# Index stacks issued from two queues, top-k and splits spread over the attention units, and dummy products in its short units

## The chip, the cores and the metric

One core of a Trainium2 chip runs the whole program as one launch. The metric is the device time of one execution in microseconds; lower is better.

## What is computed

Two blocks on 512 tokens of width 1024, in float32. The first block has two layers of feed-forward, hybrid mixer, output product and feed-forward, each with a layer norm; the second is a Mamba-2 and RG-LRU block with a feed-forward. The change touches the hybrid mixer alone, which runs once in each of the two layers. Of it, cut to what matters here:

```python
def dsa_mixer(q, k, v, q_idx, k_idx, w_idx, ...):      # per block of 128 queries
    rel = jax.nn.relu(jnp.einsum('bqhd,bsd->bqhs', qi, k_idx))   # 8 index heads of 32
    score = jnp.einsum('bqh,bqhs->bqs', wi, rel)
    score = jnp.where(k_pos <= q_pos, score, NEG_INF)
    _, idx = lax.top_k(score, 128)                      # then attention on the chosen keys
...
y = concatenate([mla(...), nsa(...), dsa(...), stick_breaking(...)])   # 4 heads of 64 each
```

## The kernel before

Every large product is made of three float32r products: a high part (`whi`, copied by ACT, L314) and a low part (`wlo`, subtracted on DVE, L318) of the weights, which come through a ring of four `raw` buffers that SP loads (L302). One weight tile is a slot. PE's slot needs both parts of its tile, and ACT and DVE make those of slot n+2 while PE works on slot n.

**The front** (`mixer_front`, phase "proj") has 20 slots: 12 feature tiles, 4 token tiles (12 to 15), and 4 feature tiles (16 to 19) whose matmuls (L1058 to L1060) (24 a slot) are interleaved with index scores (L1030, 6 a slot, 24 in all): stack of head h by `kstack`, then a relu on ACT (L1147) into `rel`, then a weighted sum on DVE (L1223, L1227) into `picked` (named idx_score in the trace). For each of the 8 index heads the stack holds four copies of 32 rows, high, low, high, low, of the rotated queries; SP makes them with four transfers a head, 32 in a layer (L931): heads 0 to 3 at its step 12, heads 4 to 7 at its step 14. `rel` lies on the memory of the queries' high parts, so the first relu waits until the second half of the stacks has landed (`istack_in1`). The first half must have landed before PE's first index product. In its last two slots ACT and DVE also make the high and low parts of the next phase's first two tiles, and DVE ends with three additions of the causal mask to the score blocks (L1252).

**Attention** (`mixer_attention`, phase "att") is a list of 20 groups of 4 units (heads), 80 units, in the order of `ORDER`; a unit belongs to one of five kinds and one block of 128 queries. On every unit the engines do, each in its own order: PE the scores of unit u+2 (L1370, mask L1371), the transposes of unit u (L1380), the values of u-1 (L1391); DVE the row minimum of u+2 (L1560); ACT the exponential of u+1 (L1472) and the copy of the transposed probabilities of u (L1481). PE's `transposes(u)` waits first for `pt_done`, the copy of unit u-1, then for `exp_done`; on ACT that copy comes behind the exponential of u. 16 steps of stick-breaking attention (L1408 to L1429) are spread over the units. DVE also makes the 48 top-k rounds, one each on units 0 to 47, in the order of blocks 1, 2, 3: `max` finds the eight largest (L1537), `match_replace` takes them out (L1544). ACT and DVE split 12 operand tiles into high and low parts, one a unit on units 0 to 11 (L1457, L1459; L1597, L1600). A block's choice is needed by its DSA group: block 2 at unit 48, block 3 at 64, block 1 at 76. Units of a "cmp" group have a width of 31 keys, those of block 0 a width of 128. `keep_clock` (L369) exists and isn't called before the change.

Of the kernel before, what the change touches and what calls it, by code (L numbers as in the profile page):

```python
# [7 lines left out]
F32 = mybir.dt.float32  # L8
# [6 lines left out]
P = 128  # L15
# [826 lines left out]
def mixer_front(c, m, l, following):  # L842
# [24 lines left out]
    index = (IDXK, IDXQ, IDXQ + 1)  # L867
# [8 lines left out]
    def halves(lo, hi, dim):  # L876

        half = dim // 2
        return [(a, a + half if (a - lo) // half % 2 == 0 else a - half, half) for a in range(lo, hi, half)]

# [5 lines left out]
    with ExitStack() as ctx:  # L886
# [5 lines left out]
        with nc.Block() as block:  # L892
            @block.sync
            def _(sp):
# [40 lines left out]
                for n in range(slots):  # L935
# [31 lines left out]
                    if n == 14:  # L967
# [3 lines left out]

                        sp.wait_ge(ph["gelu_done"], 2)
                        stack(1)
# [6 lines left out]
            def _(pe):  # L980
# [89 lines left out]
                for n in range(2, slots):  # L1070
# [14 lines left out]
            def _(act):  # L1085
# [41 lines left out]
                def index_hi(i):  # L1127
                    if i == 0:
                        act.wait_ge(ph["idxk_in"], 64)
                    else:  # L1130
                        act.wait_ge(ph["rope_done"], parts[order.index(4 + i) + 1])
                    hi, _, src, _ = m.split[index[i]]
                    act.activation(hi, src, ACT.Copy).then_inc(ph["ihi_done"], 1)
                    if i == 0:
                        act.wait_ge(ph["copies_in"], 16 * 6)
                        act.activation(kstack[0:64], src[0:64], ACT.Copy).then_inc(ph["ihi_done"], 1)

                def relus(n):
                    for i in rels_of(n):
# [4 lines left out]
                        if i >= 3:  # L1144
# [6 lines left out]
                          11: lambda: (index_hi(2), gelus()), 12: compressed}  # L1151
                act.nop().then_inc(ph["bank_free"], 4)
                apply.act(act)
                for n in range(slots):
# [4 lines left out]
                    ph.hi(act, n // 4, n % 4, width(n + 2), last=n >= slots - 4)  # L1159
# [4 lines left out]
            def _(dve):  # L1164
# [36 lines left out]
                def index_lo(i):  # L1201
                    dve.wait_ge(ph["ihi_done"], i + 2)
                    hi, lo, src, _ = m.split[index[i]]
                    if i == 0:
# [27 lines left out]
                for n in range(slots):  # L1232
# [5 lines left out]
                    ph.lo(dve, n // 4, n % 4, width(n + 2), last=n >= slots - 4)  # L1238
# [10 lines left out]
                dve.wait_ge(ph["acc_done"], len(rels))  # L1249
# [1337 lines left out]
```

## Time and profile before

| | |
|---|---|
| median of 3 runs | 3546.96 us (3545.58 to 3554.99) |
| the profiled execution's own time | 3556.16 us |
| its span | 3554.3 us |
| mean granted TensorE clock | 0.967 of full |
| fronts: layer 0, layer 1 | about 400 to 555 us, about 1553 to 1709 us |
| attention: layer 0, layer 1 | about 555 to 724 us, about 1709 to 1871 us |

The span runs from the first to the last instruction that the profile shows; the execution's own time has 1.9 us around it. A granted clock of 1.00 is 2.4 GHz on TensorE, 0.50 is 1.2 GHz. Attention is counted here from ACT's first copy of transposed probabilities to its last: 560.92 to 724.05 us and 1714.24 to 1870.84 us. Unit 8 of layer 1 begins by the same mark at 1732.24 us, unit 48 at 1814.88 us. A matmul's end is modelled, so a matmul that is issued every 0.22 us is shown as lasting 0.39 us.

### The profile page before, as it was taken

How to read it: one execution, taken by the hardware profiler on the slowest of the kernel's cores; microseconds unless marked ns; L12 is line 12 of the kernel's file. 1: busy time of each engine (PE TensorE's matmuls, PEld its weight loads, DVE VectorE, ACT ScalarE, POOL GpSimd, SP SyncE). 2: the span in 40 equal slices, each digit the busy share in tenths (PEclk: the TensorE clock that was granted, in tenths of full speed). 3: DMA queues.
4: the chain of work that ended last, by engine and by line, in shares of the span. 5: the costliest groups of instructions: out<-in, count | busy, mean ns of one | idle time of the engine just before them, and what ended most of it. 6: DMA issues, size and time to landing. Idle time of an engine off the chain costs nothing. (4 is left out here: it accounts for less than half of the span.)

```text
span 3554.3 us, 41810 instructions
## 1 busy us (share of the span) xinstructions
PE 3322.8 (93%) x15368; PEld 2671.0 (75%) x15370; DVE 1642.7 (46%) x2465; ACT 1413.4 (40%) x2342; POOL 77.5 (2%) x52
## 2 busy tenths in 40 slices
PE   7999988989999999999898999979999899889998
PEld 5887776768888788777676888847777677768886
DVE  3333457753333433345865333366566346343333
ACT  4332436544322433243665332245555237233321
POOL 0001000010001000100001000100000000000000
PEclk9999998999999999999999999989999999999999
DMA  3232240012232233224001223211111222222231
GB/s 133 97 107 98 90 121 24 1 60 89 95 106 85 74 96 103 98 90 122 24 1 60 95 99 104 81 56 55 55 66 61 76 81 103 77 72 99 94 107 65
DMA packets 85880, 286.34 MB, mean 81 GB/s; under 512 B 15841, under 2 KB 19425, under 8 KB 85217
## 3 DMA queue, kind: packets, MB, share of 16 engines
q1 hardware_dynamic: 85728, 284.37, 24.3%
q8 instruction: 89, 1.46, 0.2%
q14 instruction: 63, 0.51, 0.0%
HBM read 269.12 MB, written 2.10 MB: 76 GB/s over the span
## 5 line engine op out<-in xcount | busy, mean ns | idle before, releaser
L318 DVE TENSOR_TENSOR wlo<-raw,whi 128x1024 fp32r<-128x1024 f32 (+3 forms) x464 | 609.3, 1313 | 989.0 <-ACT whi L314 988.8
L346 PE MATMUL ps<-xh,whi 128*128 128x512 f32 x2256 | 886.1, 393 | 16.7 <-DVE xl L2535 6.3
L347 PE MATMUL ps<-xl,whi 128*128 128x512 f32 x2256 | 880.1, 390 | 0.0
L348 PE MATMUL ps<-xh,wlo 128*128 128x512 f32 x2256 | 879.9, 390 | 0.0
L314 ACT ACTIVATE whi<-raw 128x1024 fp32r<-128x1024 f32 (+3 forms) x464 | 515.0, 1110 | 657.6 <-PE ps L348 614.3
L346 PEld LDWEIGHTS ps<-xh,whi 128*128 128x128 f32 x2256 | 425.2, 188 | 114.8 <-issue 25.1
L348 PEld LDWEIGHTS ps<-xh,wlo 128*128 128x128 f32 x2256 | 425.0, 188 | 88.7
L347 PEld LDWEIGHTS ps<-xl,whi 128*128 128x128 f32 x2256 | 425.1, 188 | 88.6 <-issue 1.7
L346 PE MATMUL ps<-ffn_hh,whi 128*128 128x512 f32 x880 | 347.2, 395 | 11.1 <-DVE ffn_hl L751 11.1
L347 PE MATMUL ps<-ffn_hl,whi 128*128 128x512 f32 x880 | 345.1, 392 | 0.0
L348 PE MATMUL ps<-ffn_hh,wlo 128*128 128x512 f32 x880 | 345.0, 392 | 0.0
L706 ACT ACTIVATE ffn_hh<-ffn_gate 128x512 f32 (+1 forms) x110 | 69.6, 633 | 512.0 <-DVE ffn_gate L749 512.0
L749 DVE TENSOR_TENSOR ffn_gate<-ffn_gate,ps 128x512 f32<-128x512 f32 x110 | 75.7, 688 | 282.6 <-PE ps L348 282.6
L346 PEld LDWEIGHTS ps<-ffn_hh,whi 128*128 128x128 f32 x880 | 166.8, 189 | 48.8 <-DVE ffn_hl L751 13.2
L347 PEld LDWEIGHTS ps<-ffn_hl,whi 128*128 128x128 f32 x880 | 166.8, 190 | 35.5 <-issue 1.0
L348 PEld LDWEIGHTS ps<-ffn_hh,wlo 128*128 128x128 f32 x880 | 166.7, 189 | 35.0
L1950 PE MATMUL ps<-xh,whi 128*128 128x512 f32 x384 | 159.9, 416 | 15.8 <-PEq L297 15.8
L702 ACT ACTIVATE ffn_gate<-ps 128x512 f32<-128x512 f32 x110 | 65.9, 599 | 257.1 <-PE ps L348 254.4
L1951 PE MATMUL ps<-xl,whi 128*128 128x512 f32 x384 | 152.8, 398 | 0.0
L1952 PE MATMUL ps<-xh,wlo 128*128 128x512 f32 x384 | 152.5, 397 | 0.0
L509 POOL TENSOR_TENSOR x<-x,mean_rest 128x512 f32<-128x512 f32 x48 | 77.3, 1644 | 2173.0 <-ACT mean_rest L473 2173.0
L751 DVE TENSOR_TENSOR ffn_hl<-ffn_gate,ffn_hh 128x512 f32 (+1 forms) x110 | 76.2, 693 | 98.8 <-ACT ffn_hh L706 98.8
(393 smaller groups left out, 4095.5 us busy)
## 6 DMA issues: line engine op xcount, KB each, us to landing
raw<-in_ffn_up SPq DMA_DIRECT2D x216, 512.0 KB, 3.5
raw<-in_ffn_down SPq DMA_DIRECT2D x80, 704.0 KB, 4.0
raw<-in_ssm_in SPq DMA_DIRECT2D x44, 512.0 KB, 3.5
raw<-in_mix_in SPq DMA_DIRECT2D x32, 512.0 KB, 3.6
raw<-in_lru_in SPq DMA_DIRECT2D x20, 512.0 KB, 3.6
raw<-in_mix_out SPq DMA_DIRECT2D x16, 512.0 KB, 3.7
raw<-in_ssm_out SPq DMA_DIRECT2D x16, 512.0 KB, 3.5
raw<-in_lru_out SPq DMA_DIRECT2D x8, 640.0 KB, 3.9
```

Of the source, the lines that this page charges most:

```text
L314: act.activation(self.core.whi[:, u % HALF, 0:width], self.core.raw[:, u, 0:width], ACT.Copy).then_inc(sems["hi_done"], 1)
L318: dve.tensor_tensor(self.core.wlo[:, u % HALF, 0:width], self.core.raw[:, u, 0:width], self.core.whi[:, u % HALF, 0:width].bitcast(F32), A ...
L346: pe.matmul(out, c.whi[:, h, w], xh[:, k0 + k], start=first and k == 0, stop=False)
L347: pe.matmul(out, c.whi[:, h, w], xl[:, k0 + k], start=False, stop=False)
L348: mm = pe.matmul(out, c.wlo[:, h, w], xh[:, k0 + k], start=False, stop=last and k == nk - 1)
L509: pool.tensor_tensor(c.x[:, t], c.x[:, t], c.dneg[:], ALU.add).then_inc(ph["xc_done"], 1)
L706: act.activation(hh[:, p], gate[:, u // 2], ACT.Copy).then_inc(ph["hh_done"], 1)
L749: dve.tensor_tensor(gate[:, u // 2], gate[:, u // 2], c.ps[:, u], ALU.mult).then_inc(ph["prod_done"], 1)
L751: dve.tensor_tensor(hl[:, p], gate[:, u // 2], hh[:, p].bitcast(F32), ALU.subtract).then_inc(ph["hl_done"], 1)
L1950: pe.matmul(out, c.whi[:, h, w], c.xh[:, t], start=t == 0, stop=False)
L1951: pe.matmul(out, c.whi[:, h, w], c.xl[:, t], start=False, stop=False)
L1952: mm = pe.matmul(out, c.wlo[:, h, w], c.xh[:, t], start=False, stop=t == DT - 1)
```

## The change

It lets ACT issue the stacks of heads 0 to 3 (one at its step 12, two at 13, one at 14) and SP those of heads 6, 7, 4, 5 (steps 12, 13, 14), and splits the index queries before the index key. It leaves out the next phase's first two tiles in the front's last two slots and makes them on attention's units 34 and 36. It moves the three mask additions to units 3, 5 and 7. It takes the top-k blocks in the order 2, 3, 1, with the 48 rounds spread evenly over units 9 to 70. It keeps the first seven splits on units 0 to 6 and puts the other five on units 20, 23, 26, 29 and 31. And it puts dummy products (bf16, 512 columns) into `transposes`, between its two waits: two on a unit with a width under 128, one on a unit with a width of 128.

```diff
-    index = (IDXK, IDXQ, IDXQ + 1)
+    index = (IDXQ, IDXQ + 1, IDXK)
 ...
+    def stack_head(engine, h):
+        hi, lo = m.split[IDXQ + h // 4][:2]
+        rows = slice(32 * (h % 4), 32 * (h % 4) + 32)
+        for g in range(4):
+            engine.dma_start(stack_of[h][32 * g:32 * g + 32].bitcast(F32), (hi, lo)[g % 2][rows, P:SEQ].bitcast(F32)).then_inc(ph[f"istack_in{h // 4}"], 16)
 ...
-                def stack(i):
-                    sp.wait_ge(ph["ilo_done"], i + 2)
-                    t = IDXQ + i
-                    hi, lo = m.split[t][0], m.split[t][1]
-                    for h in range(4):
-                        rows = slice(32 * h, 32 * h + 32)
-                        for g in range(4):
-                            sp.dma_start(stack_of[4 * i + h][32 * g:32 * g + 32].bitcast(F32), (hi, lo)[g % 2][rows, P:SEQ].bitcast(F32)).then_inc(ph[f"istack_in{i}"], 16)
+                def stack(heads):
+                    for h in heads:
+                        stack_head(sp, h)
 ...
                     if n == 12:
-                        sp.wait_ge(ph["km_done"], HEADS)
-                        sp.wait_ge(ph["vm_done"], 2)
-                        stack(0)
                         sp.wait_ge(ph["rope_done"], parts[order.index(9) + 1])
                         for a in (0, 64):
                             sp.dma_start(m.h[a:a + 64, KWIN], m.h[64:P, KSLC]).then_inc(ph["kwin_in"], 16)
 ...
                     if n == 14:
                         sp.wait_ge(ph["kwin_in"], 32)
                         sp.dma_start(m.h[64:P, KSLC], m.h[0:64, KSLC]).then_inc(ph["kslc_in"], 16)
+                        stack((4, 5))
+                    if n == 12:
+                        sp.wait_ge(ph["ilo_done"], 2)
+                        stack((6,))
+                    if n == 13:
                         sp.wait_ge(ph["gelu_done"], 2)
-                        stack(1)
+                        stack((7,))
 ...
-                            pe.wait_ge(ph["ilo_done"], 1)
+                            pe.wait_ge(ph["ilo_done"], 3)
 ...
+                def stack(h):
+                    act.wait_ge(ph["ilo_done"], 1)
+                    act.wait_ge(ph["km_done"], HEADS)
+                    act.wait_ge(ph["vm_done"], 2)
+                    stack_head(act, h)
 ...
-                          11: lambda: (index_hi(2), gelus()), 12: compressed}
+                          11: lambda: (index_hi(2), gelus()), 12: lambda: (compressed(), stack(0)),
+                          13: lambda: (stack(1), stack(2)), 14: lambda: stack(3)}
 ...
-                    ph.hi(act, n // 4, n % 4, width(n + 2), last=n >= slots - 4)
+                    if n + 2 < slots:
+                        ph.hi(act, n // 4, n % 4, width(n + 2))
 ...
-                    ph.lo(dve, n // 4, n % 4, width(n + 2), last=n >= slots - 4)
+                    if n + 2 < slots:
+                        ph.lo(dve, n // 4, n % 4, width(n + 2))
 ...
-                dve.wait_ge(ph["acc_done"], len(rels))
-                for b in range(1, QB):
-                    own = m.picked[b][:, b * P:(b + 1) * P]
-                    dve.tensor_tensor(own, own, c.k["negd"], ALU.add).then_inc(ph["acc_done"], 1)
 ...
-    rounds = [(b, r) for b in range(1, QB) for r in range(TOPK // 8)]
+    chosen = (2, 3, 1)
+    rounds = [(b, r) for b in chosen for r in range(TOPK // 8)]
+    round_at = {9 + k * (n - 19) // (len(rounds) - 1): k for k in range(len(rounds))}
+    done_at = {b: max(u for u, k in round_at.items() if rounds[k][0] == b) for b in chosen}
 ...
+    part_at = dict(zip((0, 1, 2, 3, 4, 5, 6, 20, 23, 26, 29, 31), range(len(parts))))
+    ahead_at = {34: 0, 36: 1}
 ...
-                    for b in range(1, QB):
+                    for b in chosen:
                         if u == first_unit[2, b]:
-                            pe.wait_ge(ph["choice_done"], b)
+                            pe.wait_ge(ph["choice_done"], chosen.index(b) + 1)
 ...
                     if u >= 1:
                         pe.wait_ge(ph["pt_done"], u)
+                    keep_clock(c, pe, T_BANK, 2 if x["width"] < P else 1 if x["width"] == P else 0)
                     pe.wait_ge(ph["exp_done"], u + 1)
 ...
-                    if u < len(parts):
-                        hi(u)
+                    if u in part_at:
+                        hi(part_at[u])
+                    if u in ahead_at:
+                        ph.split_hi(act, c.sides[0], 0, ahead_at[u], D)
 ...
+                def own_block(b):
+                    own = picked[b][:, b * P:(b + 1) * P]
+                    dve.tensor_tensor(own, own, c.k["negd"], ALU.add).then_inc(ph["own_done"], 1)
 ...
-                    largest()
+                    if u in (3, 5, 7):
+                        own_block((3, 5, 7).index(u) + 1)
+                    if u in round_at:
+                        largest(round_at[u])
                     if u % HEADS == 1 and u > HEADS:
                         finish(u // HEADS - 1)
-                    take()
-                    if u < len(parts):
-                        lo(u)
-                    allow()
+                    if u in round_at:
+                        take(round_at[u])
+                    if u in part_at:
+                        lo(part_at[u])
+                    if u in ahead_at:
+                        ph.split_lo(dve, c.sides[0], 0, ahead_at[u], D)
+                    if u in round_at:
+                        allow(round_at[u])
```

## Rows read from the trace of the kernel before

**Rows 1.** The page, part 1: busy time and share of the span by engine.

```profile
PE 3322.8 (93%) x15368; PEld 2671.0 (75%) x15370; DVE 1642.7 (46%) x2465; ACT 1413.4 (40%) x2342; POOL 77.5 (2%) x52
```

**Rows 2.** Waits from 330 to 560 us: who waited for whom, total, times, longest.

```profile
ACT idx_rel L1147 <- DMA idx_stack<-mix_h_split: 11.9, 1, 11.9
...
PE ps L1030 <- ACT idx_rel L1147: 8.8, 1, 8.8
```

**Rows 3.** Timeline of the SP queue, layer 0: start us, us, engine, line, transfer.

```profile
499.16 0.51 SPq L931 DMA_DIRECT2D idx_stack<-index_hi  x1
...
508.58 0.59 SPq L931 DMA_DIRECT2D idx_stack<-mix_h_split  x1
...
514.00 1.78 SPq L931 DMA_DIRECT2D idx_stack<-index_hi  x1
...
523.43 0.59 SPq L931 DMA_DIRECT2D idx_stack<-mix_h_split  x1
```

**Rows 4.** Transfers into idx_stack: min, median and max from issue to landing.

```profile
DMA to landing us min/median/max: 1.9/1.9/3.5
```

**Rows 5.** Timeline of ACT, front of layer 0.

```profile
502.24 0.99 ACT L314 ACTIVATE whi<-raw 128x936 fp32r<-128x936 f32 x1 [4.57 <-PE ps L1044]
...
512.48 1.06 ACT L314 ACTIVATE whi<-raw 128x1024 fp32r<-128x1024 f32 x1 [4.06 <-PE ps L1044]
...
530.85 0.60 ACT L1158 ACTIVATE mix_h<-ps 128x512 f32<-128x512 f32 x1 [1.96 <-PE ps L1060]
...
550.69 0.60 ACT L1158 ACTIVATE mix_h<-ps 128x512 f32<-128x512 f32 x1 [0.76 <-PE ps L1060]
```

**Rows 6.** Timeline of PE, the same stretch.

```profile
513.02 0.39 PE L1059 MATMUL ps<-xl,whi 128*128 128x512 f32 x1
513.24 0.39 PE L1060 MATMUL ps<-xh,wlo 128*128 128x512 f32 x1
...
525.86 0.69 PE L1030 MATMUL ps<-idx_kstack,idx_stack 128*128 128x384 f32 x1 [8.79 <-ACT idx_rel L1147]
```

**Rows 7.** Windows at half clock: us, busy PE, PEld, DVE, ACT, POOL; clock, DMA share, GB/s.

```profile
526.00:531.00 5.00, 5.00 (x12) 3.98 (x13) 2.81 (x6) 2.08 (x6) 0.00 (x0) 0.50 0.49 186
583.00:597.00 14.00, 14.00 (x62) 12.16 (x62) 8.98 (x31) 6.56 (x23) 0.00 (x0) 0.50 0.05 11
1771.00:1780.00 9.00, 9.00 (x43) 8.14 (x43) 7.05 (x23) 3.68 (x15) 0.00 (x0) 0.50 0.01 2
```

**Rows 8.** Timelines of DVE and ACT at the front's end and after it.

```profile
511.81 2.30 DVE L1214 COPY mix_tok_sb<-ps 128x468 f32<-128x468 f32 x4
...
553.40 0.69 DVE L1252 TENSOR_TENSOR idx_score<-idx_score,consts_sb 128x128 f32<-128x128 f32 x3
...
555.49 1.28 ACT L1509 ACT_TABLE_LOAD   x1 [3.26 <-PEq L297]
```

**Rows 9.** Windows of attention: both layers, then layer 1 in three parts.

```profile
560.92:724.05 163.13, 148.83 (x966) 123.02 (x966) 118.09 (x340) 98.46 (x314) 0.00 (x0) 0.90 0.03 8
1714.24:1870.84 156.60, 141.83 (x966) 116.79 (x966) 117.87 (x340) 98.12 (x314) 0.00 (x0) 0.95 0.03 8
1714.24:1732.24 18.00, 14.58 (x87) 9.81 (x86) 17.48 (x49) 14.80 (x43) 0.00 (x0) 0.97 0.13 31
1732.24:1814.88 82.64, 73.67 (x505) 62.10 (x506) 75.89 (x221) 47.82 (x156) 0.00 (x0) 0.93 0.03 8
1814.88:1870.84 55.96, 53.58 (x375) 44.88 (x375) 24.50 (x72) 35.49 (x118) 0.00 (x0) 0.97 0.00 1
```

**Rows 10.** Top-k instructions on idx_score (ns min/median/max), and one split on DVE.

```profile
L1537 DVE MAX8 idx_top<-idx_score x96: 371/552/696, 560.8 to 1814.4; 128x8 f32<-128x256 f32 x32, 128x8 f32<-128x384 f32 x32, 128x8 f32<-128x512 f32 x32
...
L1544 DVE MATCH_REPLACE8 idx_score<-idx_top,idx_score x96: 408/542/678, 561.4 to 1815.2; 128x256 f32<-128x256 f32 x32, 128x384 f32<-128x384 f32 x32, 128x512 f32<-128x512 f32 x32
...
568.92 0.69 DVE L1597 SCALAR_TENSOR_TENSOR mix_h_split<-mix_h,query_stack 64x512 fp32r<-64x512 f32 x1
```

**Rows 11.** Waits in layer 1's attention.

```profile
PE ps L1380 <- ACT att_pt L1481: 11.0, 16, 1.7
```

More of the change, by code:

```diff
@@ L1127, in index_hi @@
                 def index_hi(i):
-                    if i == 0:
+                    hi, _, src, _ = m.split[index[i]]
+                    if index[i] == IDXK:
                         act.wait_ge(ph["idxk_in"], 64)
                     else:
-                        act.wait_ge(ph["rope_done"], parts[order.index(4 + i) + 1])
-                    hi, _, src, _ = m.split[index[i]]
+                        act.wait_ge(ph["rope_done"], parts[order.index(5 + i) + 1])
                     act.activation(hi, src, ACT.Copy).then_inc(ph["ihi_done"], 1)
-                    if i == 0:
+                    if index[i] == IDXK:
                         act.wait_ge(ph["copies_in"], 16 * 6)
                         act.activation(kstack[0:64], src[0:64], ACT.Copy).then_inc(ph["ihi_done"], 1)
+                def stack(h):
[3 more added lines that the diff above has]
+                    stack_head(act, h)
                 def relus(n):
@@ L1201, in index_lo @@
                 def index_lo(i):
-                    dve.wait_ge(ph["ihi_done"], i + 2)
+                    dve.wait_ge(ph["ihi_done"], i + 1)
                     hi, lo, src, _ = m.split[index[i]]
-                    if i == 0:
+                    if index[i] == IDXK:
                         hi, lo, src = hi[64:P], kstack[64:P], src[64:P]
@@ L1320, in mixer_attention @@
         first_unit.setdefault(g["mixer"], HEADS * k)
-    assert all(first_unit[2, b] >= b * (TOPK // 8) + 4 for b in range(1, QB)), "one round a unit"
+    assert len(round_at) == len(rounds) and all(first_unit[2, b] >= done_at[b] + 4 for b in chosen), "the choice comes in time"
     shortened = lambda x: x["width"] < P
@@ L1336, in mixer_attention @@
                    "gexp_done gsum_done gates_done pt_done pv_done part_done y_done top_done took_done choice_done "
-                   "zero_done nsaq_in dsaq_in z_done abs_done e_done l_done spraw_done sp_done after_done a_done spv_done sy_done")
+                   "own_done zero_done nsaq_in dsaq_in z_done abs_done e_done l_done spraw_done sp_done after_done a_done spv_done sy_done")
         with nc.Block() as block:
@@ L1528, in _, with largest, take, allow @@
             def _(dve):
-                took, allows = [0], [0]
-                def largest():
-                    if took[0] < len(rounds):
-                        b, r = rounds[took[0]]
-                        if took[0]:
-                            dve.wait_ge(ph["took_done"], took[0])
-                        dve.max(top8, picked[b]).then_inc(ph["top_done"], 1)
-                def take():
-                    if took[0] < len(rounds):
-                        b, r = rounds[took[0]]
-                        took[0] += 1
-                        dve.wait_ge(ph["top_done"], took[0])
-                        dve.match_replace(picked[b], top8, picked[b], TAKEN).then_inc(ph["took_done"], 1)
-                def allow():
-                    if took[0] and rounds[took[0] - 1][1] == TOPK // 8 - 1 and took[0] // (TOPK // 8) > allows[0]:
-                        b = rounds[took[0] - 1][0]
-                        allows[0] += 1
-                        dve.wait_ge(ph["took_done"], took[0])
+                def own_block(b):
+                    own = picked[b][:, b * P:(b + 1) * P]
+                    dve.tensor_tensor(own, own, c.k["negd"], ALU.add).then_inc(ph["own_done"], 1)
+                def largest(k):
+                    b, r = rounds[k]
+                    dve.wait_ge(ph["own_done"], QB - 1)
+                    if k:
+                        dve.wait_ge(ph["took_done"], k)
+                    dve.max(top8, picked[b]).then_inc(ph["top_done"], 1)
+                def take(k):
+                    b, r = rounds[k]
+                    dve.wait_ge(ph["top_done"], k + 1)
+                    dve.match_replace(picked[b], top8, picked[b], TAKEN).then_inc(ph["took_done"], 1)
+                def allow(k):
+                    b, r = rounds[k]
+                    if r == TOPK // 8 - 1:
+                        dve.wait_ge(ph["took_done"], k + 1)
                         dve.tensor_scalar(allowed[b], picked[b], TAKEN, NEG, ALU.not_equal, ALU.mult).then_inc(ph["choice_done"], 1)
```

## The prediction

> **What bounds the kernel now.** The busy shares come first: PE 93%, DVE 46%, ACT 40% [rows 1]. PE is the bound, so time can only be won where PE stands still, runs at half clock, or is paced by another engine. The waits of a mixer front name one large hole: ACT's first relu waits 11.9 us for the stack transfers, and PE's fifth index product 8.8 us for that relu [rows 2]. The SP queue says why they are late: its 32 stack issues run from 499.16 to 524.0 us, 0.63 us apart (499.16 to 508.58 is 15 steps), one of them 1.78 us long [rows 3]. A transfer lands 1.9 us after its issue, and in most cases no later [rows 4]: the issuing is slow, not the moving.
>
> What the hole costs is read on ACT. Slot 16 begins at 512.48 and ends at 530.85, 18.4 us; the next three of its sort take 6.6 each (530.85 to 550.69) [rows 5]. That is 11.8 us too much: PE stands until 525.86 [rows 6], and then works at a granted clock of 0.50 to 531 [rows 7]. Layer 1 shows the same hole in the same form.
>
> Behind the last relu the front's end is ACT's and DVE's: ACT has evacuated at 551.29 [rows 5], DVE ends the mask additions at 554.09, and attention's first ACT instruction starts at 555.49 [rows 8], 1.4 us after.
>
> Attention takes 163.1 us in layer 0 and 156.6 in layer 1 with the same instructions. In layer 1, DVE is busy 17.5 of 18.0 us in units 0 to 7, 75.9 of 82.6 in units 8 to 47, and 24.5 of 56.0 in units 48 to 79, where PE is busy 53.6 [rows 9]. So DVE paces the first 48 units and PE, with the latency of its chain through DVE and ACT, the last 32. On top, PE stands at 0.50 clock from 583 to 597 us in layer 0 and from 1771 to 1780 in layer 1 [rows 7]; layer 1 has nothing like the first stretch, which is the 6.5 us between the layers.
>
> **The change, part by part** (each layer unless said).
>
> *Stacks from two queues.* SP's share falls from 32 issues to 16. It starts as before at 499.16 and has 19 issues and one weight load left, 20 x 0.63 = 12.6 us, so it ends at 511.8, or 513.3 with 1.5 us held at the load for DVE's slot 15; landed by 515.2. The first relu then waits until 515.2 and not until 525.4. PE comes to its fifth index product at 525.86 - 8.79 = 517.07 [rows 6], so this wait is gone. What is late next is ACT. Its 16 issues have no row in this trace. From below they cost nothing, from above 1.78 us each [rows 3]; I take SP's common 0.63. ACT works about 1 us in a token slot of 5.12 (502.24 to 512.48 is two) [rows 5]. One head (2.5 us) fits into slot 12; two heads at step 13 (5.0 us behind a split that ends at 503.3) end at 508.3 and push the split of slot 16 from 507.4 (502.24 + 5.12) by 0.9 us. Behind it DVE has the low part, three query operations and the token copies that PE waits for, which begin at 511.81 [rows 8]: about 0.9 us late, and PE with them. Head 3 is issued by 511.9 and lands by 513.8, about when PE's first index product wants it. Remaining loss in slot 16: 0.4 us of today's normal restart plus 0.9, so about 1.3 of the 11.8. Gain 10.5, twice **21.0 us**. At 1.0 us an issue ACT's last stack lands near 518, and some 3 us a layer of this gain are lost; at 1.78 for all, near 530, which is 4.5 us a layer worse than today (3541 in the sum for the median). SP shows that length once, so I leave that end out of the range.
>
> The transfers themselves are the place to weigh a rule. In the 5 us behind the hole the DMA share is 0.49 [rows 7] with one queue's issues; two queues double the rate of stack issues, so the 16 engines would be near full at worst, and the landing of 1.9 us [rows 4] may grow by a microsecond, which I leave in the range. The Trainium skill ("DMA: Bandwidth & Descriptors", Issuing engines are not separate DMA queues) says that several issuers share the same 16 engines and save only the sequencer's time, usually small beside the transfer. By that rule taken strictly the front's 21.0 us would be near 0 and the sum 15 us; the trace speaks against it, because here the sequencer's time, 0.63 us an issue, is what ends last.
>
> *Moving the key's split behind the queries'* costs nothing: its low part comes at DVE's step 13 instead of 10, three slots ahead of PE's first index product, and that is its cover; were it gone, PE would wait for one operation of 0.7 us.
>
> *Front's end.* Without two splits and three additions the last work is ACT's evacuation, 551.29 instead of 554.09 [rows 5, 8]: 2.8 us, twice **5.6 us**.
>
> *Attention, rounds and splits.* A round is MAX8 plus MATCH_REPLACE8 plus some 0.09 us: 0.37 + 0.41 for block 1, 0.55 + 0.54 for block 2, 0.70 + 0.68 for block 3 [rows 10], so 0.87, 1.18 and 1.47 us. Units 0 to 7 lose 8 rounds (7.0 us) and a stacked split (two of 0.69 [rows 10], 1.4), and get three additions (0.9): DVE 17.5 to 10.0. ACT, 14.8 less 1.3 of the split, is next, with PE at 14.6 plus dummies. I take 15.3 for 18.0: gain 2.7. Units 8 to 47 change 40 rounds for 31 (8 of block 1 and one of block 3 less, 8.4 us), get the split of unit 7 (1.4) and the next phase's two (2.4): DVE 75.9 to 71.3. Units 48 to 79 get 17 rounds, 1.5 + 16 x 0.87 = 15.4: DVE 24.5 to 39.9 of 56, still under PE; a round may hold up a row minimum now and then, bounded by 0 and 15.4 us; I take 0.7, since the minimum runs two units ahead of PE's transposes.
>
> *Dummies.* 16 units of two and 16 of one, 48 a layer. A 512-column product is issued every 0.22 us (513.02 to 513.24) [rows 6], so 10.6 us of PE a layer, 1.8 of it in units 48 to 79. They stand behind the wait for ACT's copy and ahead of the one for the exponential. All of PE's waits there (11.0 us) are put down to the copy [rows 11], which comes behind the exponential on ACT, so nothing hides them at that place; they are hidden only where DVE paces the unit. They can give back what half clock costs: 6.5 us in layer 0, and in layer 1's 1771 to 1780 (layer 0 has its like) 9 us at 0.50, half of it at most, 4.5; I take 2.3, since DVE is busy 7.05 of those 9 [rows 7]. For units 8 to 47 the ends are 82.6 less the DVE relief, the clock and no price for dummies, 75.7, and PE 73.7 + 7.9 - 4.5 = 77.1 plus today's excess over the bound (82.6 - 75.9 = 6.7), 83.8. I take 81.3, nearer the second: gain 1.3. In units 48 to 79 they cost 1.8.
>
> Attention of layer 1: 2.7 + 1.3 - 0.7 - 1.8 = 1.5 us won. Layer 0: the same and the 6.5 of its first half-clock stretch, which PE's fuller units 0 to 11 should keep away: 8.0. Together **9.5 us**.
>
> **Sum:** 21.0 + 5.6 + 9.5 = 36.1 us off 3556.2, so 3520.1 for this profiled execution. It stands 9.2 us over the median of 3546.96. The half-clock stretch of 6.5 us that only one layer shows is the kind of thing that comes in some executions; the median likely has less of it, so of the median I take off 21.0 + 5.6 + 3.0 and some 3 for it: 32.6 us, **3514.4**.
>
> **Rivals.** *The clock and DVE's relief bring more:* dummies lie beside DVE-paced work and both layers run warm at unit lengths near the larger of the two engines. For it: DVE is busy 97% in units 0 to 7. Against: rows 11. Units 8 to 47 at 75.7 are 5.6 a layer better, 11.2 in all: 3503.
> *The dummies don't do what they are put there for*, or cost all 10.6 us: half clock stays and attention gains nothing or loses up to 6 a layer. For it: they sit behind the wait that binds. Then 26.6 us less 0 to 12: 3520 to 3532.
> *The front stays bound by its transfers or by ACT's issues* (1.0 to 1.5 us each, or landing slower by several microseconds): 10 to 20 of the 21 are lost, 3524 to 3535. Against: SP's steady 0.63. The Trainium skill's section on issuing engines, named above, points to this case.
> *Slower:* every round and dummy set into attention lands on the chain scores, minimum, exponential, transposes, and the early units give nothing back: 15.4 + 10.6 = 26.0 us a layer, 52.0, less the front's 26.6, so 3547 + 25 = 3572. It decides from 13.3 us of growth a layer. Against: DVE is busy 24.5 of 56 us where the rounds go, and 7 us leave units 0 to 7.
>
> **How the numbers follow.** A measurement tells 0.3%, 10.6 us, from no change: 3536.3 and 3557.6. Chances: forecast 0.60, more 0.15, dummies in vain 0.12 (0.02 of it beyond 3536), transfers or ACT's issues 0.09 (0.03 beyond), slower 0.04 (half of it past 3557.6). Faster 0.91, same 0.07, slower 0.02. The range takes the first rival to 3498 (its 3503 and the whole 4.5 of clock once more) and the dear ends to 3531.
>
> **What would show it.** Right: no wait of ACT for idx_stack above 2 us; slot 16 between two ACT marks at 7 to 9 us; 16 stack issues a layer on ACT at about 0.6 us; ACT's first attention instruction 1.4 us after the evacuation; DVE near 10 us in units 0 to 7 and no granted clock of 0.50 in them; units 48 to 79 at 57 to 59 us. Wrong: a wait of PE for `tok_out` or the first stacks of several microseconds, slots 13 to 15 longer than 5.2 us, units of the "cmp" groups longer than before at full clock, or att_least late in units 48 to 70.

## The result and the profile after

| | before | after |
|---|---|---|
| median | 3546.61 us (4 runs, 3545.58 to 3554.99) | 3516.89 us (4 runs, 3516.47 to 3517.36) |
| the profiled execution's own time, span | 3556.16, 3554.3 | 3516.91, 3515.1 |
| mean granted TensorE clock | 0.967 | 0.974 |

The ratio is 0.9911, 95% interval 0.9894 to 0.9928: 29.7 us faster by the medians. The forecast was 3514.4 with a range of 3498 to 3531.

**The front.** Part 1 of the page has as much work as before [rows 1], and the 78 more PE records that the dummies leave (their 96 weight loads are all there: 15466 against 15370):

```profile
PE 3314.9 (94%) x15446; PEld 2662.7 (76%) x15466; DVE 1643.6 (47%) x2465; ACT 1414.3 (40%) x2342; POOL 77.5 (2%) x52
```

The waits from 400 to 560 us, where rows 2 had 11.9 us of ACT and 8.8 of PE, have one row for the stacks left:

```profile
ACT idx_rel L1157 <- DMA idx_stack<-mix_h_split: 2.7, 1, 2.7
```

The timeline of ACT and its queue (ACTq) in the same stretch, to be read beside rows 5 and 8:

```profile
497.52 0.61 ACTq L886 DMA_DIRECT2D idx_stack<-index_hi  x1
...
502.82 0.53 ACTq L886 DMA_DIRECT2D idx_stack<-index_hi  x1
...
507.24 0.62 ACTq L886 DMA_DIRECT2D idx_stack<-mix_h_split  x1
507.96 1.06 ACT L314 ACTIVATE whi<-raw 128x1024 fp32r<-128x1024 f32 x1 [4.24 <-PE ps L1048]
508.07 0.54 ACTq L886 DMA_DIRECT2D idx_stack<-index_hi  x1
508.63 0.61 ACTq L886 DMA_DIRECT2D idx_stack<-mix_h_split  x1
...
512.98 1.06 ACT L314 ACTIVATE whi<-raw 128x1024 fp32r<-128x1024 f32 x1 [3.96 <-PE ps L1048]
516.75 2.66 ACT L1157 ACTIVATE idx_rel<-ps 128x256 f32<-128x256 f32 x6 [2.71 <-DMA idx_stack<-mix_h_split]
520.17 0.60 ACT L1169 ACTIVATE mix_h<-ps 128x512 f32<-128x512 f32 x1 [0.76 <-PE ps L1064]
...
539.85 0.60 ACT L1169 ACTIVATE mix_h<-ps 128x512 f32<-128x512 f32 x1 [0.76 <-PE ps L1064]
541.84 1.28 ACT L1524 ACT_TABLE_LOAD   x1 [1.39 <-PEq L297]
```

Slot 16, counted as before from the split that opens it to the evacuation that ends it, takes 512.98 to 520.17, 7.2 us for 18.4. The two heads of step 13 end at 507.86 and the split behind them starts at 507.96; the next comes 5.02 us later, at 512.98, so ACT's issues hold up nothing that PE waits for. At the other end, the evacuation ends at 540.45 and attention's table load starts 1.39 us after; before it was 551.29 and 555.49, 4.20 after [rows 5, 8]. That is 2.8 us a layer.

SP's half of the issues, and what the tile's answer says of all of them (durations in ns, then the landing):

```profile
501.01 0.60 SPq L886 DMA_DIRECT2D idx_stack<-index_hi  x1
...
513.45 0.59 SPq L886 DMA_DIRECT2D idx_stack<-mix_h_split  x1
```

```profile
L886 ACTq DMA_DIRECT2D idx_stack<-index_hi x16: 524/610/623, 497.5 to 1641.6; - x16
...
L886 SPq DMA_DIRECT2D idx_stack<-index_hi x16: 590/597/709, 501.0 to 1645.1; - x16
...
DMA to landing us min/median/max: 1.9/3.1/4.6
```

ACT issues at SP's price, 0.61 us. The landing grew from a median of 1.9 [rows 4] to 3.1 us. SP's last issue starts at 513.45 and the first relu, which waits for its transfer, at 516.75, 3.3 us later. A landing of 1.9 us would have ended this wait at 515.35, so about 1.4 of the 2.7 us are the slower landing, and the rest is that the issues end late.

**Attention.** Windows of both layers, then of layer 1 in the three parts of rows 9, then of the stretch at half clock in layer 0 (columns as in rows 7):

```profile
547.01:702.50 155.49, 146.78 (x1005) 120.40 (x1014) 121.55 (x345) 100.41 (x317) 0.00 (x0) 0.96 0.03 8
1678.35:1829.48 151.13, 141.82 (x1005) 116.11 (x1014) 120.89 (x345) 100.18 (x316) 0.00 (x0) 1.00 0.04 8
1678.35:1692.11 13.76, 12.78 (x86) 9.63 (x86) 10.52 (x26) 12.40 (x39) 0.00 (x0) 0.98 0.17 41
1692.11:1773.84 81.73, 75.86 (x543) 61.81 (x548) 71.98 (x197) 52.18 (x162) 0.00 (x0) 1.00 0.03 8
1773.84:1829.48 55.64, 53.18 (x381) 44.68 (x382) 38.39 (x124) 35.60 (x118) 0.00 (x0) 1.00 0.00 1
597.00:610.00 13.00, 11.60 (x60) 10.31 (x61) 10.20 (x33) 6.52 (x20) 0.00 (x0) 0.62 0.10 22
```

Units 0 to 7 have lost 4.2 us, units 8 to 47 0.9, units 48 to 79 0.3. In layer 1 the granted clock is at 1.00 nearly throughout; in layer 0 there is still a stretch at half clock, later than before. How much of this is the dummies' work, and at what price, these windows don't say: that is what the experiments are for.

### The profile page after: what moved, and what is told of

Read it like the earlier page. It is cut to its first block and busy times, and to the rows that moved or that the text cites. A ratio compares the mean times of both kernels' runs of the same rounds, so it can differ in the third digit from the quotient of the medians.

```text
span 3515.1 us, 42066 instructions
## 1 busy us (share of the span) xinstructions
PE 3314.9 (94%) x15446; PEld 2662.7 (76%) x15466; DVE 1643.6 (47%) x2465; ACT 1414.3 (40%) x2342; POOL 77.5 (2%) x52
## 5 line engine op out<-in xcount | busy, mean ns | idle before, releaser
L346 PE MATMUL ps<-xh,whi 128*128 128x512 f32 x2256 | 886.1, 393 | 17.1 <-DVE xl L2558 6.3
L749 DVE TENSOR_TENSOR ffn_gate<-ffn_gate,ps 128x512 f32<-128x512 f32 x110 | 75.6, 687 | 282.2 <-PE ps L348 282.2
```

Source lines behind the costliest of these rows:

```text
L346: pe.matmul(out, c.whi[:, h, w], xh[:, k0 + k], start=first and k == 0, stop=False)
L749: dve.tensor_tensor(gate[:, u // 2], gate[:, u // 2], c.ps[:, u], ALU.mult).then_inc(ph["prod_done"], 1)
```

## The experiments

Each kernel was timed in 3 rounds beside the kernel before on the same chip, in three sets on three chips. The kernel before had a median of 3548.39 us beside the first three changed kernels of the table, 3549.78 beside the four with a shifted start and 3547.98 beside the last four. "Attention" is the length of both layers in the profiled execution, first to last of ACT's copies, with the granted clock of each.

| kernel | median (range) us | ratio [95% interval] | attention us (clock) |
|---|---|---|---|
| the kernel before again | 3546.43 (3542.76 to 3551.22) | 0.9999 [0.9989, 1.0009] | 155.0, 156.1 (0.96, 0.96) |
| before + new stacks | 3525.61 (3522.67 to 3534.32) | 0.9944 [0.9927, 0.9961] | 155.0, 155.0 (0.96, 0.96) |
| after, all stacks on SP | 3531.10 (3528.60 to 3534.33) | 0.9957 [0.9939, 0.9974] | 154.2, 154.3 (0.98, 0.98) |
| after, no dummies | 3508.70 (3505.30 to 3509.79) | 0.9891 [0.9874, 0.9908] | 155.7, 152.4 (0.93, 0.96) |
| after, shifted start, short | 3519.11 (3511.95 to 3523.91) | 0.9925 [0.9908, 0.9941] | 155.5, 154.4 (0.96, 0.98) |
| after, shifted start, long | 3519.86 (3517.83 to 3525.20) | 0.9924 [0.9908, 0.9941] | 154.4, 155.5 (0.98, 0.96) |
| no dummies, shifted, short | 3506.24 (3501.95 to 3509.00) | 0.9882 [0.9865, 0.9898] | 152.4, 152.4 (0.96, 0.96) |
| no dummies, shifted, long | 3509.16 (3508.36 to 3510.48) | 0.9893 [0.9877, 0.9910] | 150.3, 150.3 (0.97, 0.97) |
| no dummies, front's end back | 3516.33 (3508.08 to 3517.20) | 0.9906 [0.9889, 0.9923] | 150.3, 150.6 (0.96, 0.96) |
| no dummies, splits back | 3508.76 (3504.81 to 3516.76) | 0.9899 [0.9882, 0.9916] | 148.1, 151.0 (0.98, 0.96) |
| after, double dummies | 3526.77 (3522.51 to 3532.00) | 0.9944 [0.9927, 0.9961] | 162.3, 157.7 (0.97, 1.00) |
| before + new stacks + dummies | 3530.68 (3530.04 to 3531.04) | 0.9954 [0.9937, 0.9970] | 157.3, 157.4 (0.96, 0.97) |

### The kernel before once more

No edit. The prediction took 6.5 us of layer 0's attention for a half-clock stretch that layer 1 did not have.

> The kernel before, unchanged, for a second profile. Theory: the stretch of 0.50 clock from unit 8 on in layer 0 (6.5 us between the layers) is not a property of the kernel but comes in some executions; then this profile's own time may lie near 3546, and attention of layer 0 at 156 to 157 us. Rival: it is there each time at the same units; then 163 us again and a time near 3556 for every profiled execution.

Windows of its attention, and of the units that stood at 0.50 in rows 7:

```profile
557.92:712.94 155.02, 141.46 (x967) 115.64 (x965) 117.75 (x340) 98.30 (x315) 0.00 (x0) 0.96 0.03 8
1700.34:1856.40 156.06, 140.39 (x967) 115.22 (x966) 117.74 (x340) 98.09 (x314) 0.00 (x0) 0.96 0.03 8
580.00:594.00 14.00, 13.34 (x97) 10.99 (x95) 13.45 (x43) 9.50 (x31) 0.00 (x0) 1.00 0.05 12
```

The same kernel has no such stretch here, and its layer 0 takes 155.0 and not 163.1 us. It belongs to an execution, not to the kernel, so removing it is no gain of the change. The fair base for attention is 155 to 156 us in both layers.

### The stacks alone

The kernel before with the change's order of the index tiles and its stacks on two queues, and nothing else:

```diff
-    index = (IDXK, IDXQ, IDXQ + 1)
+    index = (IDXQ, IDXQ + 1, IDXK)
...
-                        11: lambda: (index_hi(2), gelus()), 12: compressed}
+                        11: lambda: (index_hi(2), gelus()), 12: lambda: (compressed(), stack(0)),
+                        13: lambda: (stack(1), stack(2)), 14: lambda: stack(3)}
```

> The kernel before with only the stacks issued from ACT and SP (index queries split first). Theory: slot 16 of the front falls from 18.4 to about 7.2 us in each layer, nothing else changes, so 22 us off: 3522 to 3527. Rival (what the front wins is lost again in attention, since the time is paced by DVE there): under 12 us off, above 3535.

It took 3525.61 us where the kernel before took 3546.43 and, over all its runs on that chip beside it, 3548.39: 21 to 23 us less. Its timeline of ACT has slot 16 as the changed kernel has it, 7.2 us:

```profile
511.25 1.06 ACT L314 ACTIVATE whi<-raw 128x1024 fp32r<-128x1024 f32 x1 [3.95 <-PE ps L1048]
...
518.47 0.60 ACT L1169 ACTIVATE mix_h<-ps 128x512 f32<-128x512 f32 x1 [0.77 <-PE ps L1064]
...
542.96 1.28 ACT L1520 ACT_TABLE_LOAD   x1 [3.27 <-PEq L297]
```

11.2 us a layer off slot 16, 22.4 in all, is the whole of the difference. Nothing was given back in attention (155.0 twice). The order of the index tiles and the issues on ACT cost nothing that shows.

### One queue or two

The changed kernel with all 32 stack issues on SP, at the same steps:

```diff
-                         stack((4, 5))
+                         stack((3, 4, 5))
...
-                         stack((6,))
+                         stack((0, 6))
...
-                         stack((7,))
+                         stack((1, 2, 7))
...
-                           ... 12: lambda: (compressed(), stack(0)),
-                        13: lambda: (stack(1), stack(2)), 14: lambda: stack(3)}
+                           ... 12: compressed}
```

> The changed kernel with all 32 stack transfers on SP, at the changed kernel's steps 12 to 14. Theory (the issuing queue's time is what ends last): SP needs 32 x 0.63 = 20 us from about 501, lands near 524, slot 16 is again 16 to 18 us: 3535 to 3540. Rival (it was the order and the earlier steps that won, not the second queue): 3517 to 3524.

It took 3531.10 us, 14.2 more than the changed kernel. That is some 4 less than the theory's lower end and 7 above the rival's upper one. The waits, ACT's timeline and one window of layer 0:

```profile
ACT idx_rel L1159 <- DMA idx_stack<-mix_h_split: 11.1, 1, 11.1
```

```profile
513.61 1.06 ACT L314 ACTIVATE whi<-raw 128x1024 fp32r<-128x1024 f32 x1 [4.06 <-PE ps L1050]
525.77 1.92 ACT L1159 ACTIVATE idx_rel<-ps 128x256 f32<-128x256 f32 x5 [11.10 <-DMA idx_stack<-mix_h_split]
...
529.42 0.60 ACT L1170 ACTIVATE mix_h<-ps 128x512 f32<-128x512 f32 x1 [0.76 <-PE ps L1066]
```

```profile
526.00:531.00 5.00, 5.00 (x24) 4.16 (x23) 2.90 (x7) 3.87 (x9) 0.00 (x0) 0.97 0.51 197
```

The old wait is back, but slot 16 takes 15.8 us and not 18.4. The first relu starts 12.2 us after the slot opens, before it was 12.9; from that relu to the slot's end it is 3.65 us, before it was 5.43. With the new order PE stops earlier and is back earlier: it waits 5.9 us for the last of the first four stacks, works again from 520.65, and has a granted clock of 0.97 from 526 to 531, where the kernel before has 0.50 [rows 7]. So the second queue is worth 8.6 us a layer in the slot (15.8 less 7.2), and the rest of the 11.2 goes with the order of the stacks. Issuing was what ended last. The slots of both layers show 17 us and the time shows 14. Most of the rest is in how attention starts: from ACT's table load to its first copy are 3.46 us in each layer with all stacks on SP, at a granted clock of 1.00, and 5.17 and 4.24 in the changed kernel, at 0.53 and 0.65. The Trainium skill ("DMA: Bandwidth & Descriptors", Issuing engines are not separate DMA queues) has it that a second issuer saves the sequencer's time only, usually small beside the transfer. The first half agrees with these runs: what was saved is the time of the issues. The second does not: one issue of 0.6 us is a third of a landing of 1.9 us, and in a burst the issues add up while the landings overlap, so 32 of them, 20 us, are ten times the landing of one, and taking half of them away brought 14 us.

### Without the dummies

```diff
-                    keep_clock(c, pe, T_BANK, 2 if x["width"] < P else 1 if x["width"] == P else 0)
```

> The changed kernel without its dummy products. Theory (the dummies pay about what they cost: PE work of 10.6 us a layer, part of it beside DVE's, against half-clock stretches): 3510 to 3524, with some granted clock of 0.50 in units 0 to 40. Rival 1 (the dummies keep the clock and are what attention's gain comes from): 3525 to 3532, attention of layer 1 near 156 us. Rival 2 (they are in vain): 3500 to 3509, no more half clock than now.

3508.70 us: 8.2 faster than the changed kernel, and the fastest so far. That is below the theory's range and within that of rival 2, but rival 2 wanted no more half clock than now, and there is more. The clock is lower (0.93 and 0.96) and the attention of the profiled execution no shorter, so one start of each could be an accident of where the half clock falls. To rule that out the start of the program was shifted, by one product of 256 or 512 columns ahead of the first real ones, into a bank that nobody reads there:

```diff
+                pe.matmul(c.ps[:, 2, 0:256], c.k["ident"], c.x[:, 4, 0:256], start=True, stop=True)
```

It was done with and without the dummies.

> The changed kernel with one idle product of 256 columns ahead of the first real one, which moves all that follows by 0.5 to 0.9 us. Theory A (where the half-clock stretches fall hangs on when the stages begin, so the 8 us between the changed kernel and the one without dummies hold several us of chance): the time moves by more than the delay, by 2 to 8 us either way, 3509 to 3524. Theory B (the dummies cost 8 us of their own): 3517 to 3518.

> The same with one product of 512 columns, 0.9 to 1.8 us later. Theory A: 3509 to 3525, and not the time of the short delay. Theory B: 3518 to 3519.

> The changed kernel without dummies with the short delay. Theory A: 3503 to 3520. Theory B: 3509 to 3510. If the mean over the three starts is lower without dummies by 4 us or more, they cost; if it is within 3 us, they are neutral.

> The same without dummies with the long delay. Theory A: 3503 to 3520. Theory B: 3510 to 3511.

Over the three starts, the twelve runs with dummies lie between 3511.95 and 3525.20, mean 3518.7; the twelve without between 3501.95 and 3510.48, mean 3507.8. The two sets don't overlap, and on the one chip that ran all four shifted kernels, eight runs against eight, the difference is 12.0. By the rule put on record (4 us or more) **the dummies cost 11 us.** Theory A's numbers held only in their wide ranges: the medians moved by 2.2 and 3.0 us with dummies and by 2.5 the other way and 0.5 without, and the two delays with dummies differ by 0.8, not by several us. Theory B's ranges were each missed, by 0.8 to 2.8 us. Windows of the kernel without them (long shift) for both layers and for layer 1's three parts:

```profile
545.91:696.23 150.32, 137.10 (x967) 112.73 (x966) 120.78 (x345) 99.43 (x316) 0.00 (x0) 0.97 0.03 8
1672.31:1822.61 150.30, 137.10 (x967) 112.71 (x966) 120.72 (x345) 99.42 (x317) 0.00 (x0) 0.97 0.04 8
1672.31:1685.75 13.44, 12.81 (x83) 9.36 (x82) 10.46 (x26) 12.25 (x38) 0.00 (x0) 0.95 0.18 41
1685.75:1767.83 82.08, 71.97 (x513) 59.55 (x512) 72.01 (x197) 51.81 (x163) 0.00 (x0) 0.96 0.03 8
1767.83:1822.61 54.78, 52.32 (x376) 43.80 (x374) 38.26 (x124) 35.35 (x118) 0.00 (x0) 1.00 0.00 1
```

Beside the changed kernel's layer 1 this is the trade. With dummies the clock is 1.00 and PE is busy 141.8 us; without them it is 0.97, with a stretch at half clock left, PE is busy 137.1 us, and the layer is 0.8 us shorter. The changed kernel's other layer, and both of the two shifted kernels, have dummies and half clock together (0.96 to 0.98) and take 154.4 to 155.5.

These lengths hang on where attention is said to begin. Without dummies, short shift and then long shift, layer 0 from ACT's table load to its first copy, and then units 0 to 7:

```profile
542.34:545.80 3.46, 3.42 (x15) 1.87 (x15) 2.15 (x5) 3.13 (x8) 0.00 (x0) 1.00 0.00 0
545.80:562.04 16.24, 15.06 (x82) 10.99 (x80) 10.79 (x25) 12.43 (x39) 0.00 (x0) 0.79 0.15 34
540.50:545.91 5.41, 5.38 (x13) 3.03 (x14) 2.13 (x6) 3.27 (x7) 0.00 (x0) 0.50 0.00 0
545.91:559.35 13.44, 12.80 (x83) 9.36 (x82) 10.47 (x26) 12.26 (x39) 0.00 (x0) 0.95 0.18 41
```

A stretch of some 7 us at half clock lies behind the first copy in the one and mostly ahead of it in the other. Counted from the table load to the last copy, five of the six layers without dummies take 155.7 to 155.8 us and one 159.2. With dummies the one layer at a clock of 1.00 takes 155.4, and the five others 157.8 to 160.7; the means are 156.3 and 158.9. So in the one layer where the dummies hold the clock throughout they break even, and where they don't, a layer is 2 to 5 us longer.

Where the 48 products go is read from the waits of layer 1's attention. The changed kernel:

```profile
PEld ps L1395 <- ACT att_pt L1496: 8.1, 15, 1.3
ACT att_pt L1496 <- PE ps L1395: 8.1, 17, 1.1
PE ps L1395 <- ACT att_pt L1496: 6.0, 11, 1.2
```

Without dummies (long shift):

```profile
PEld ps L1395 <- ACT att_pt L1496: 14.5, 24, 1.9
PE ps L1395 <- ACT att_pt L1496: 9.6, 14, 1.8
ACT att_pt L1496 <- PE ps L1395: 5.2, 12, 0.9
```

PE's own wait in front of the transposes shrinks by 3.6 us (9.6 to 6.0), and ACT's wait for these transposes grows by 2.9 (5.2 to 8.1): a dummy in front of the transpose holds back what ACT copies next. Over all six layers of each sort PE's wait falls from a mean of 9.6 to 5.3 us and ACT's grows from 6.4 to 11.3.

Over all profiled executions of this family the attention takes 154.4 us a layer with dummies (six layers) and 151.6 without (eight, with the kernel whose splits are back): 5.7 of the 11 us for the two layers. The rest is spread over stretches that the edit doesn't touch, 2.1 us of it behind the second attention; what makes it is not settled.

### Twice the dummies

```diff
-                    keep_clock(c, pe, T_BANK, 2 if x["width"] < P else 1 if x["width"] == P else 0)
+                    keep_clock(c, pe, T_BANK, 4 if x["width"] < P else 2 if x["width"] == P else 0)
```

> The changed kernel with twice the dummy products: four in the units of fewer than 128 rows, two in those of 128. Theory: the first set costs some 11 us over the two layers, at full clock and nearly all on TensorE's chain, so a second set costs as much or more: 3526 to 3534. Rival: with more of them the half clock in attention goes, or they lie in TensorE's idle time: 3520 or less.

3526.77 us, 8.1 over the mean of the kernels with the single set, at the lower edge of what the theory gave; the rival falls. Windows of its attention, and the wait of ACT in layer 1:

```profile
544.44:706.69 162.25, 155.66 (x1053) 124.07 (x1062) 122.09 (x345) 101.41 (x317) 0.00 (x0) 0.97 0.03 8
1683.06:1840.80 157.74, 151.46 (x1053) 120.58 (x1062) 121.48 (x345) 101.24 (x317) 0.00 (x0) 1.00 0.03 8
```

```profile
ACT att_pt L1496 <- PE ps L1395: 17.0, 31, 1.3
```

In attention the second set costs 5.6 us a layer (160.0 against 154.4), twice what the first does there: it finds less idle time left to lie in (PE's wait for the copy is down to 4.2 us), and it does not free layer 0 of half clock either. ACT's wait for the transposes is 17.0 us for 8.1. The whole kernel shows less of it, 8.1 us where the two layers show 11.2; the difference is not explained.

### The dummies with the old rounds and splits

The kernel before with the stacks of the change and its dummies:

```diff
+                    keep_clock(c, pe, T_BANK, 2 if x["width"] < P else 1 if x["width"] == P else 0)
```

> The kernel before with the stacks of the changed kernel and its dummy products, and with the old order of rounds and splits in attention and the old end of the front; the same without dummies took 3525.6 us. Theory: there VectorE and ScalarE set the pace of the units to 47, so the dummies lie mostly in TensorE's idle time, and they cost 4 us at most: 3522 to 3530. Rival: they cost as much as in the changed kernel, some 11 us: 3533 to 3540.

3530.68 us, 5.1 over the same kernel without dummies, which is between the theory's 4 at most and the rival's 11. Attention grew by 2.3 us a layer, 4.7 for the two, nearly as much as in the changed kernel (2.8). By attention, then, the dummies are hidden little better where VectorE has all its old work in the early units. By the whole time they cost half as much (5.1 against 11), and that difference lies outside attention and is not explained, so how much the cover by VectorE is worth stays open.

### The front's end back

No dummies; the next phase's two splits and the three mask additions where the kernel before had them:

```diff
-                    if n + 2 < slots:
-                        ph.hi(act, n // 4, n % 4, width(n + 2))
+                    ph.hi(act, n // 4, n % 4, width(n + 2), last=n >= slots - 4)
...
-    ahead_at = {34: 0, 36: 1}
+    ahead_at = {}
...
-                    if u in (3, 5, 7):
-                        own_block((3, 5, 7).index(u) + 1)
```

> The changed kernel without its dummy products, and with the two splits of the next phase's weights and the three mask additions back where the kernel before had them, at the end of the front and on every unit. Against the kernels without dummies so far (3507.8 us over twelve runs). Theory: what leaves the front's end comes back into the chain there (the attention's table load 2.8 us later in each layer), and attention gets nothing for it: 3511 to 3516. Rival: it is neutral, since what attention is spared is as long: 3509 or less.

3516.33 us against 3508.48, the median of the twelve runs without dummies: 7.9 us dearer, 0.3 above the theory's range, and the rival falls (one of its four runs was at 3508.08, so the size is rough; by the means it is 6.7). Its timeline of ACT, layer 0:

```profile
540.13 0.60 ACT L1169 ACTIVATE mix_h<-ps 128x512 f32<-128x512 f32 x1 [0.76 <-PE ps L1064]
540.63 1.05 ACT L314 ACTIVATE whi<-raw 128x1024 fp32r<-128x1024 f32 x1
544.94 1.28 ACT L1525 ACT_TABLE_LOAD   x1 [3.27 <-PEq L297]
```

From the evacuation's end at 540.73 to the table load are 4.2 us, in the changed kernel 1.39: the 2.8 a layer of the prediction, 5.6 in all. The rest is within the spread of the runs. The attention, without the two splits and three additions, is 150.3 and 150.6 us, and from the table load to the last copy 155.6 and 156.0. Five of the six layers that make these splits and additions themselves, without dummies, have 155.7 to 155.8: where the splits went they cost about nothing.

This kernel also differs from the one with the new stacks alone in nothing but the spread of rounds and output splits. It is 9.3 us faster (3516.33 against 3525.61), and its attention 4.55 us a layer shorter (155.0 to 150.3 and 150.6), 9.1 in all. That is what the spreading brings.

### The splits back

No dummies; the twelve output splits on units 0 to 11 as before, the rounds spread:

```diff
-    part_at = dict(zip((0, 1, 2, 3, 4, 5, 6, 20, 23, 26, 29, 31), range(len(parts))))
+    part_at = dict(zip(range(12), range(len(parts))))
```

> The changed kernel without its dummy products, and with the twelve splits of the output weights back on units 0 to 11; the top-k rounds stay spread. Theory: in units 0 to 11 VectorE has rounds and splits together, and the spread rounds are what brings the relief, so 3508 to 3513. Rival: the splits carry the relief of units 0 to 11, and their return costs all that the spreading brought: 3516 or more.

3508.76 us, as without the edit and within the theory's range. Layer 0's attention is even the shortest of all, 148.1 us. By the starts of ACT's copies units 0 to 7 take 15.8 and 15.6 us in the two layers, in place of 13.4, and units 8 to 47 77.5 and 80.6 in place of 82.1. That a split moved from unit 7 to unit 31 is paid for there is read from these lengths alone, and the granted clock of units 8 to 47 differs too (0.98 and 0.94 for 0.96). Of the two things spread over attention it is the rounds that shorten it.

## Why the prediction was right, and where it was off

**The sign and the size.** The median was to fall by 32.6 us and fell by 29.7. By parts, from the runs: stacks 21 to 23 (predicted 21.0), front's end 5.6 in the trace and 7 to 8 in the time (predicted 5.6), rounds and splits some 9, and dummies some 11 the other way. Stacks and front's end, by the trace 22.4 and 5.6, leave 1.7 of the 29.7 for attention as a whole (predicted 6.0 of the median, 9.5 of the profiled execution). The parts taken from different runs add up only within a few microseconds. The error lies in attention.

**Stacks from two queues.** Right in mechanism and in price. SP was to start at 499.16 and to end its issues at 511.8 to 513.3; it started at 501.01, behind two window copies that now come first, and ended at 514.04. ACT's issues were put at 0.63 us and took 0.61. Two further terms were off and cancelled, which is luck. The landing grew by 1.2 us, which the prediction named and left in the range, and the first relu begins at 516.75 and not at 515.2. The 0.9 us by which ACT's issues were to push the split of slot 16 did not come: ACT's queue issues while ACT executes (the ACTIVATE of 507.96 runs beside the issues of 508.07 and 508.63), and the split of 507.96 came 5.22 us after the one before it, 0.1 us more than the 5.12 of before, and the next 5.02 after it. Slot 16 was put at 7.9 us and took 7.2. In the end that was left out of the range, 1.78 us for all of ACT's issues, the prediction's own terms (21.0 lost and 4.5 a layer beyond) give 3544 and not 3541.

**Units 0 to 7** were put at 15.3 us and took 13.8. DVE's 10.0 was right (10.5), but PE, put at 14.6 and its dummies, is busy 12.8 us, and ACT, put at 13.5, 12.4: both were read from a stretch that DVE had drawn out. Part of the 13.8 is chance. In the six layers with dummies these units take 13.8 to 17.1 us at granted clocks of 0.98 to 0.80, so the sign "no half clock in units 0 to 7" failed.

**Units 8 to 47**: 81.3 predicted, 81.7 measured, for a reason that is only half the one given. DVE was to be relieved by 4.6 us and was by 3.9 (75.9 to 72.0). But the units barely followed: without dummies and at 0.96 clock they still take 82.1 us, with DVE and PE busy 72.0 each, and with the old rounds and the new stacks alone they take 80.9, with DVE busy 75.6. So the step that said DVE paces the first 48 units held for units 0 to 7 alone; behind them no engine is full, and what paces them is taken to be the chain from one engine to the next, which no run isolates. The 4.55 us a layer of the spreading lie in units 0 to 7 (18.1 to 13.6) and 48 to 79 (56.1 to 54.8), less the microsecond that units 8 to 47 got longer.

**Units 48 to 79**: 58.5 predicted, 55.6 measured, 54.8 without dummies. DVE went from 24.5 to 38.4 us of work there and the units didn't lengthen; they are shorter than before (56.0), so the 0.7 us for delayed minima was too much, and the sign "57 to 59 us" was missed on the good side.

**The dummies** are the step that failed. They were costed at 1.8 us in units 48 to 79 and, through a choice between two ends, at a small net gain elsewhere. In units 48 to 79 they cost 0.9 (55.64 against 54.78). In attention as a whole they cost 2.8 us a layer and over the whole kernel 11 us. The prediction had the reason in hand, that they stand behind the wait for ACT's copy [rows 11], and gave their cost to the second rival with a chance of 0.12, as a total loss of 10.6 us a layer. What came is between: part lies in PE's idle time, part delays the transposes. They were also to keep half clock out of the first units and did not. What they were to give back is little. Half clock in the attention windows fell, worked out over windows of 5 us (twice the length times one less the clock), from 12.0 to 8.6 us a layer, and half clock costs at most half of its length, so 1.7 us.

**Layer 0's 6.5 us** were counted as a gain in the sum for the profiled execution (3520.1; it took 3516.91 from 3556.16, a fall of 39.2 for the predicted 36.1). The kernel before without that stretch shows that this was the execution's, as the prediction suspected when it took only 3 us of it for the median.

**Rivals.** The first (clock and relief bring more, 3503) is nearest to what the kernel without dummies does (3508.5), for another reason: relief without the price. The second, that the dummies are in vain, is in substance what happened to attention. The third fell with the wait of 2.7 us (the sign was 2 us at most, so it was missed by little), and the fourth with units 48 to 79.

**The better version.** The changed kernel without the call of `keep_clock` beats both: 3508.5 us, median of twelve runs over three starts, ratios 0.9882 to 0.9893 against the kernel before, and 11 us under the changed kernel by the means.

## What to carry to other kernels

A burst of small transfers on one queue is bound by its issues; count them times the issue's length, and give half to a queue whose engine is idle, since issuing ran beside that engine's own work here. Bookkeeping on an engine that is not the bound belongs in the stretch where another engine sets the pace: 17 top-k rounds moved there were free. A product that keeps a clock up has its own price at each place, so it must be timed with and without, in a dozen executions of each, before it is kept; in units of 1 to 2 us a wait of PE is not room for a dummy when the transpose behind it is what the next engine waits for.

## What the runs showed of the hardware that was not expected

- With two queues issuing at once, the landing of the same transfers grew from 1.9 to 3.1 us (medians; longest 3.5 to 4.6), while the issues kept 0.6 us. With the new order and all issues on SP it is 2.0, so it comes with the second queue and not with the order.
- The same kernel differs from execution to execution by several microseconds: ten of the kernel before lie between 3542.76 and 3551.22 us, and its layer 0 has 14 us at half clock from 583 us on in one profile and none there in another. The changed kernel's medians at three starts are 3516.9, 3519.1 and 3519.9, its profiled spans 3515.1, 3510.2 and 3519.2, and the half-clock stretches fall on other units (layer 0's attention of the changed kernel 0.96, of its long shift 0.98, layer 1's 1.00 and 0.96). Whether the idle product moves them is not shown, since they move without it too. A difference of 2 or 3 us between two kernels of this kind says nothing of the edit with four executions of each.
- The dummies did not hold the clock in every layer: one of the six attention layers with them had a clock of 1.00, the others 0.96 to 0.98; of the eight without, 0.93 to 0.98.
